# Token sums of a two-layer encoder step: 128-column products in place of 32, four tokens per layout, twelve ring rows

## The reference

```python
def peer(h, w_q, sub_keys, expert_u, expert_v):
    ...
    ids = jnp.take_along_axis(cand_i, best_j, axis=-1)
    gates = jax.nn.softmax(best_s.astype(jnp.float32), axis=-1).astype(h.dtype)
    ...
    def expert_block(args):
        xb, idb, gtb = args
        act = jax.nn.gelu(jnp.einsum('td,thkd->thk', xb, expert_u[idb]), approximate=False)
        return jnp.einsum('thk,thkd->td', gtb * act, expert_v[idb])
```

## Time and profile before

| | |
|---|---|
| median of 3 runs | 3053.32 us (3052.96 to 3055.14) |
| span of the profiled execution | 3345.7 us |
| mean granted TensorE clock in it | 0.826 |
| bytes moved | 1201 MB, 359 GB/s over the profiled span |
| PE, DVE, POOL, ACT busy | 66%, 65%, 62%, 9% |

### The profile page before, as it was taken

The page is one execution under the profiler, slowest core; times in us unless marked ns, Lnnn a source line. Parts: engine busy times, 40 slices in busy tenths (PEclk is TensorE's granted clock), DMA queues, the critical chain, the costliest instruction groups (busy, mean ns, idle before and its releaser), DMA issues.

```text
span 3345.7 us, 23941 instructions
## 1 busy us (share of the span) xinstructions
PE 2192.0 (66%) x7260; PEld 765.3 (23%) x7260; DVE 2166.7 (65%) x5654; ACT 306.1 (9%) x657; POOL 2069.9 (62%) x2196
## 2 busy tenths in 40 slices
PE   8366776557644774688955376657895627564498
PEld 6112322112212121123312122212331212110122
DVE  4868488758777767635387967864618797636500
ACT  3100111101000001010101000000010010000000
POOL 1565665666666665566665656666666665666665
PEclk9698888778877987789977687878997868776699
DMA  6799998999999999999998999999999999999998
GB/s 248 286 365 332 368 363 329 378 379 343 373 368 339 367 374 409 410 400 365 364 362 324 385 337 359 368 365 383 360 356 343 349 365 332 384 373 377 380 375 326
DMA packets 331693, 1201.37 MB, mean 359 GB/s; under 512 B 40999, under 2 KB 41385, under 8 KB 329516
## 3 DMA queue, kind: packets, MB, share of 16 engines
q0 software_dynamic: 313344, 1140.99, 89.8%
q1 hardware_dynamic: 16988, 49.42, 3.9%
q10 hardware_dynamic: 1232, 9.44, 0.7%
HBM read 1188.82 MB, written 10.87 MB: 359 GB/s over the span
## 4 chain that ended last, share of the span: by engine, by line
DVE 26%; POOL 25%; issue 15%; another core or an unknown queue 15%; PE 13%; DMA 5%; ACT 1%; DVEq 0%; ACTq 0%; POOLq 0%
POOL rows L691 25%; DVE rows L1732 11%; PE acc L1208 7%; DVE psB L1405 4%; DMA rows<-in_expert_v,idsT 2%; DMA rows<-in_expert_u,ids 2%; PE psB L1143 1%; DVE work L1493 1%; DVE work L1486 1%; DVE work L1483 1%; PE psA L1056 1%; DVE work L1527 1%; DVE work L1533 1%; DVE work L1539 1%
## 5 line engine op out<-in xcount | busy, mean ns | idle before, releaser
L1208 PE MATMUL acc<-rows,strip 128*32 128x512 f32 x4352 | 1394.8, 658 | 462.9 <-DMA rows<-in_expert_v,idsT 305.0
L1732 DVE CUSTOM_DVE_ANT_0 rows<-rows,psH 128x1024 f32<-128x1024 f32 x1088 | 1288.3, 1218 | 336.2 <-DMA rows<-in_expert_u,ids 227.6
L691 POOL DMA_INDIRECT rows<-in_expert_v,idsT x1088 | 1030.6, 947 | 619.6 <-issue 273.0
L691 POOL DMA_INDIRECT rows<-in_expert_u,ids x1088 | 1024.1, 941 | 604.0 <-issue 326.0
L1208 PEld LDWEIGHTS acc<-rows,strip 128*32 128x32 f32 x4352 | 338.7, 116 | 1431.8 <-issue 955.0
L1405 DVE SCALAR_TENSOR_TENSOR psB<-zbuf,chan,psB 128x128 f32<-128x128 f32 (+1 forms) x827 | 202.8, 328 | 21.3 <-DVE psB L1405 16.6
L999 PE MATMUL psA<-w_out_sb,hT 128*128 128x512 f32 x288 | 153.8, 680 | 47.2 <-issue 35.1
L1039 PE MATMUL psB<-w_in_sb,hT 128*128 128x512 f32 x288 | 143.8, 649 | 56.9 <-DVE hT L1386 31.1
L1143 PE MATMUL psB<-w_q_sb,hT 128*128 128x512 f32 x288 | 142.0, 643 | 57.9 <-issue 37.5
L1739 DVE TENSOR_TENSOR x_out<-acc,x_out 128x1024 f32<-128x1024 f32 x10 | 12.2, 1222 | 248.9 <-PE acc L1208 176.6
L1056 PE MATMUL psA<-w_in_sb,hT 128*128 128x512 f32 x288 | 141.5, 646 | 1.7 <-DVEq L1573 1.7
(11 more groups left out here) (227 smaller groups left out, 1403.9 us busy)
## 6 DMA issues: line engine op xcount, KB each, us to landing
rows<-in_expert_u,ids POOLq DMA_INDIRECT x1088
rows<-in_expert_v,idsT POOLq DMA_INDIRECT x1088
w_in_sb<-in_w_in SPq DMA_DIRECT2D x4, 2176.0 KB, 30.7
w_out_sb<-in_w_out SPq DMA_DIRECT2D x2, 4096.0 KB, 18.6
w_q_sb<-in_w_q SPq DMA_DIRECT2D x2, 4096.0 KB
x_out<-x_mid SPq DMA_DIRECT2D x10, 512.0 KB
w_in_sb<-in_w_in ACTq DMA_DIRECT2D x2, 2176.0 KB, 22.8
x_mid<-x_mix SPq DMA_DIRECT2D x8, 512.0 KB
```

What stands on the lines that cost most here:

```text
L691: nc.gpsimd.indirect_dma_start(out=rows[:, j, :], out_offset=None, in_=table[:, :], in_offset=bass.IndirectOffsetOnAxis(ap=index, axis=0))\
L1208: last = nc.tensor.matmul(acc[LS * a:LS * (a + 1), half:half + 512], strip[:, first:first + LS], rows[:, at % RING, half:half + 512], star ...
L1732: nc.vector.tensor_tensor_reduce(rows[:, j, :], rows[:, j, :], psH[:, :], 1.0, 0.0, ALU.mult, ALU.add, dots[:, r:r + 1]).then_inc(s_free[j ...
```

## The change

Three things. The token products take a slice of 128 columns of the strip and write to all 128 partitions of `acc`; the token's row is found by its place in the slice, and `start` and `stop` are set once for the whole of `acc` and not once for each band. The strip is laid out with a period of 128 in place of 32, and for four tokens at a time in place of eight. The ring has 12 slots in place of 13.

```diff
-RING = 13
-GROUP = 8
+RING = 12
+GROUP = 4
+WIDE = 128
...
-        strip = sb("strip", [P, (HALVES + 1) * LS])
+        strip = sb("strip", [P, (HALVES + 1) * WIDE])
...
         def laid_off(q):
-            turn, o = divmod(LS - 1 + q, LS)
-            return strip[:, LS * turn:LS * (turn + HALVES)].rearrange("p (s o) -> p s o", o=LS)[:, :, o]
+            turn, o = divmod(WIDE - 1 + q, WIDE)
+            return strip[:, WIDE * turn:WIDE * (turn + HALVES)].rearrange("p (s o) -> p s o", o=WIDE)[:, :, o]
...
-                    step(nc.scalar.copy(dst, src[:, 2 * g4:2 * g4 + 2, :]))
+                    step(nc.scalar.copy(dst, src[:, g4 * GROUP // 4:(g4 + 1) * GROUP // 4, :]))
...
-                    first = (k % 2 * GROUP + i % GROUP + 1) * LS - 1 - (QUARTERS * b if v < QUARTERED else b)
-                    start, stop = i < 4, i + 4 >= width(v)
+                    top, inner = divmod(LS * a, WIDE)
+                    row = inner + (QUARTERS * b if v < QUARTERED else b)
+                    first = (k % 2 * GROUP + i % GROUP + 1) * WIDE - 1 - row
+                    start, stop = i < 4 and inner == 0, i + 4 >= width(v) and inner + LS == WIDE
                     for half in (0, 512):
-                        last = nc.tensor.matmul(acc[LS * a:LS * (a + 1), half:half + 512], strip[:, first:first + LS],
+                        last = nc.tensor.matmul(acc[WIDE * top:WIDE * (top + 1), half:half + 512], strip[:, first:first + WIDE],
```

## The result

The changed kernel takes 3416.72 us (median of 4 runs, 3414.49 to 3417.80). In the same comparison the kernel before takes 3053.76 us. The ratio is 1.1186 (95% interval 1.1171 to 1.1202): 363 us slower. The forecast was 3340 us in a range of 3195 to 3480.

The account below looks back on a forecast made before the run. It took DMA row gathers as the bound, with PE's tokens slower than rows in token-only stretches. 3053 + 245 (320 excess less 75) + 50 + 5 - 10 = 3343, said as 3340 us; 8-in-10 range 3195 to 3480.

Parts of the forecast that it names:

- The token on PE: PE's token products: four full-width matmuls at 0.43 us, 1.72 us a token; four tokens cost 6.88 us, before 1.88.
- The need of the stretches: In 16 token-only stretches (855 tokens, 1270.8 us) PE would need 1575 us; with 16 us unusable room, excess 320 us.
- What the ring takes back: Ring slots give rows a lead in fifteen stretches: 0 to 100 us regained, taken as 5 us each, 75 us.
- Full width outside the stretches: Tokens in mixed stretches: PE has time to catch up, 2668 us needed under 3053 overall; no loss counted.
- Profile to median: Runs 9.6% shorter than the profile, laid to slower rows under the profiler; extra stretch loss 0 to 111, taken 50 us.
- The sum against the profiled execution: Whole-kernel time at the profile's pace: 3346 + 245 + 5 - 10 = 3586 us.
- Layouts: ACT's strip copies for four tokens, 232 more (46 us of ACT), mostly beside PE's tokens: 5 us loss, bounds 0 and 69.
- The ring's thirteenth slot: One slot fewer: one 1.24 us step less in each lead, already counted in the twelve; a microsecond at the start.
- Less switching: PE between token products and mixer blocks: 0.2 us per block may go, 0 to 58 us, taken as 10 us gain.
- Absorbed: Rival: most stretches wait for DVE's routing or ids anyway, only three long ones bind; 3197 us, chance 0.11.
- Clock: Rival on clock and round trips: PE stays at 0.91 clock, tokens need 145 us more; 3488 us, chance 0.14.
- Faster: Rival: PE kept busy holds 2.4 GHz, its other work shrinks, tokens hidden; 3015 us, chance 0.03.

Follow-up runs that it names:

- half-sum kernel: The changed kernel with two matmuls a token in place of four (sum columns 512 to 1023 left out): 3430.70 us, 1.0291 of the kernel before.

## Why the prediction was right, and what was off

*The token on PE* (1.72 us whatever waits, by the mixer's 0.43): right. 16 token matmuls take 6.87 us, POOL's step became 1.72 us.

*The need of the stretches* (1575 us, and 16 that help nobody): 1597.4 us after. The long stretch 248.5 by the sum, 247.3 measured; the last 220.2 and 221.8; the one of 62 tokens 107.8 and 107.5.

*What the ring takes back* (75 us): outside the 16 stretches the kernel lasted 1866.9 us before and 1811.0 after on the faster kind of chip (time of the last token's end, 3044.4 and 3408.4, less the stretches), 56 us less. On the slower chip it is 3326.7 - 1276.1 = 2050.6 against 3597.3 - 1632.8 = 1964.5: 86 us. These are sums of all that happens outside, so they compare with 75 - 5 + 10 = 80. With full width in the stretches alone, the same stretches sum to 1598.6 us and 3381.2 - 1598.6 = 1782.6 us lie outside, 84 less than before. So what was given back was sized rightly, within 4 us.

*Full width outside the stretches* was put at nothing, since PE has time there on average. That term failed: it is the difference between 84 and 56 us, and 26 us by the times of the two kernels (3390.44 and 3416.72).

*Profile to median* (50 us) is the term that was mis-sized most, and its reason was wrong. I took the 292 us for the profiler's. They are the chip's: profiled executions of this kernel agree with the runs beside them within 3 us, and a chip of the slower kind gave the rows. The stretches of before last 1177.5 us on the faster kind, not 1270.8, so 93 us of room were missing, close to the 111 of my upper end and not to the 50 that I took. The account with what was measured is 1597.4 - 1177.5 = 420 us in the stretches, less 84, plus 28 outside: 364, where 363 was measured. It must come out, since it only divides the difference of the two profiles; what it tells is where the time lies. Mine was 320 + 50 - 75 + 5 - 10 = 290. Of the 74 us between, 50 come from the stretches (420 against 370) and 28 from full width outside them, less 4 for the rest. The two misses pull the same way, and 3417 lies at the upper edge of the forecast's own range, 3260 to 3420. The term had the right sign for a wrong reason; that the wrong reason did no more harm was luck.

The reason I gave for 50, that the stretch at 2801.70 ran at POOL's step already, was true of that one (77.7 and 73.7 us). But the last one went from 177.5 to 162.1 and the long ones from 190 and 194 to 175. The sum against the profiled execution, 3586 us, is the part that was tested as it stood: 3606 us on a chip of that kind.

*Layouts* (5 us): 1 us with 32 columns, within the interval of none. In the changed kernel ACT waits 1407 us for PE there, and what waits for these layouts are PE's weight loads, for 3.9 us in all. *The ring's thirteenth slot*, put at nothing of its own, was 17 us of a slower chip's time. *Less switching* (10 us of gain): PE's 0.2 us for each block of the mixer went wholly, as the row after shows (1.71 for 1.91); with 32 columns in one band it stayed. The Trainium skill's rule in TensorEngine Tiling, Tiling Modes (Key Properties), that a change of mode drains the engine, agrees with these rows. What it is worth in time can't be told apart, since the change loses thirty times as much elsewhere.

*The rivals.* Absorbed: no; in fifteen of the 16 stretches PE was busy for 94% of the length or more, in the short ones too (28.9 us for 16 tokens with the mixer's work between). Clock: no; where PE binds its clock is 0.95 to 1.00, and the run's mean rose to 0.899. The half-sum kernel has the lower clock of that rival, where PE has less to do, not more. Faster: the condition that it named, a full-width matmul of at most 0.35 us, is not met, though what PE does beside tokens did shrink, from 765 us busy in before on the faster chip to 725.

*The signs* that were named beforehand: starts 0.43 us apart, yes; the last 128 tokens in about 220 us, 221.8; POOL's wait for PE some 350 us, no, 822 us in 858 pieces, since at a step of 1.72 it waits for every row; busy PE toward 2700, 2738.

## What to carry to other kernels

Busy time counts side-by-side matmuls once, so it can't tell whether an engine has time for them one after the other: read starts, for a block of the narrow kind and one of the wide kind. An engine's need over the whole span (here 2668 of 3053 us) says little where work comes in stretches; make the sum for each stretch against the pace at which its input comes. Where an engine gets less work than before, look at what it waits for before calling its clock the cause: in the half-sum kernel PE stood idle for DVE. And before a difference between profile and runs is put down to the profiler, look whether both are from the same chip: here it was 292 us between chips, and at most 3 on one.

## What the runs showed of the hardware

- Token products of 32, 64 and 128 columns cost the same 0.43 us for each matmul record of 128x512 in 32-bit floats at 2.4 GHz, and those of 128 columns 0.85 at 1.2 GHz. Narrow ones gain only by standing side by side: four tokens in 1.88 us with four bands, 5.35 with two (in the order 0, 0, 1, 1), 6.99 with four bands of which one is used (32 columns), 6.87 with full width. In the order 0, 0, 1, 1 no token started past a neighbour that had to wait.
- A block of four full-width matmuls between 32-column ones takes 1.91 us, between full-width ones 1.71.
- The same program takes 3054 us on one chip and 3333 and 3349 us on two others, with the same busy times; on those two POOL waits some 380 us for something that the trace does not name, on the first not at all. Whether the chip or other work on it makes the difference is not known.
- With half the token matmuls the mean granted clock fell from 0.880 (the full sum on the same chip) to 0.781. That this cost time is not shown.
- The same 247 instructions of DVE, busy for 57 to 58 us, took 60.3 us in one kernel and 85.7 in another on the same chip; the pauses between them are not explained.
